# Seven block products for eight in the up-projection of a convolutional FFN, and the FFN in two phases

## What is computed

```python
h = rms_norm(x, norm_ffn[l])
x = x + conv_ffn(h, w_up[l], conv_w[l], conv_b[l], w_down[l])
...
def conv_ffn(h, w_up, conv_w, conv_b, w_down):
    z = causal_dwconv(h @ w_up, conv_w, conv_b)      # width 3, per channel
    val, gate = jnp.split(z, 2, axis=-1)
    return (jax.nn.gelu(gate) * val) @ w_down
```

## Time and profile before

| | us |
|---|---|
| runs of the kernel (three) | 2732.2, 2735.0, 2736.9; median 2735.0 |
| profiled execution, its own time | 2736.5 |
| its span, first to last instruction | 2734.4 |
| TensorE busy | 2628.5, 12338 matmuls and transposes |
| VectorE busy | 1347.1 |
| GpSimd busy | 851.6 |
| ScalarE busy | 693.7 |

### The profile page before, as it was taken

One profiled execution on the slowest core, in us unless ns is written; L12 is line 12 of the kernel. 1 busy time (PEld: TensorE's weight loads), 2 busy tenths in 40 slices (PEclk: granted clock), 3 DMA queues, 4 the chain that ended last, 5 costly groups with the idle time before them and its releaser, 6 DMA issues.

```text
span 2734.4 us, 32749 instructions
## 1 busy us (share of the span) xinstructions
PE 2628.5 (96%) x12338; PEld 2152.5 (79%) x12338; DVE 1347.1 (49%) x1763; ACT 693.7 (25%) x1272; POOL 851.6 (31%) x448
## 2 busy tenths in 40 slices
PE   4999999999999999999999999999999999999997
PEld 3887788887888888888878878888778888888885
DVE  7924455623555555555550335563345455555555
ACT  3126214212222222222241441331232222222222
POOL 1421222531433333333323212236033333333330
PEclk9999999999999999999999999999999999999998
DMA  5342342430111111111123224335011111111111
GB/s 179 95 102 92 128 140 96 148 114 24 62 47 46 46 46 46 46 46 46 65 84 109 70 99 149 111 123 185 1 47 53 48 46 48 52 46 47 52 46 61
DMA packets 87375, 211.34 MB, mean 77 GB/s; under 512 B 15048, under 2 KB 32232, under 8 KB 87288
## 3 DMA queue, kind: packets, MB, share of 16 engines
q1 hardware_dynamic: 47504, 127.02, 14.4%
q10 hardware_dynamic: 39784, 83.10, 8.7%
HBM read 172.87 MB, written 37.22 MB: 77 GB/s over the span
## 4 chain that ended last, share of the span: by engine, by line
PE 89%; DVE 6%; ACT 2%; issue 2%; ACTq 0%; DMA 0%; DVEq 0%; SPq 0%
PE ps L332 28%; PE ps L334 28%; PE ps L333 27%; DVE z L1214 2%; DVE act_lo L936 1%; ACT z L833 1%; PE ps L1467 1%; PE ps L1453 1%; DVE xres L1233 1%; PE ps L1402 1%; PE ps L1391 1%; PE ps L1470 1%; PE ps L1468 1%; PE ps L1318 0%; DVE glu_y L1170 0%
## 5 line engine op out<-in xcount | busy, mean ns | idle before, releaser
L332 PE MATMUL ps<-act_hi,w_hi 128*128 128x512 f32 x2240 | 883.1, 394 | 15.3 <-DVE act_lo L936 11.4
L334 PE MATMUL ps<-act_hi,w_lo 128*128 128x512 f32 x2240 | 875.8, 391 | 0.0
L333 PE MATMUL ps<-act_lo,w_hi 128*128 128x512 f32 x2240 | 875.1, 391 | 0.0
L458 POOL CAST w_hi<-w_raw 128x1024 fp32r<-128x1024 f32 x164 | 184.0, 1122 | 1778.3 <-PE ps L334 1736.7
L332 PEld LDWEIGHTS ps<-act_hi,w_hi 128*128 128x128 f32 x2240 | 422.9, 189 | 106.6 <-DVE act_lo L936 13.0
L334 PEld LDWEIGHTS ps<-act_hi,w_lo 128*128 128x128 f32 x2240 | 422.6, 189 | 89.5
L333 PEld LDWEIGHTS ps<-act_lo,w_hi 128*128 128x128 f32 x2240 | 423.1, 189 | 86.3
L1214 DVE SCALAR_TENSOR_TENSOR z<-pre,conv_v,z 128x1024 f32<-128x1024 f32 x88 | 180.1, 2047 | 523.8 <-ACT z L833 523.8
L460 POOL TENSOR_TENSOR w_lo<-w_raw,w_hi 128x1024 fp32r<-128x1024 f32 x164 | 423.7, 2584 | 13.1
L1233 DVE TENSOR_TENSOR xres<-xres,ps 128x512 f32<-128x512 f32 x352 | 232.7, 685 | 125.2 <-PE ps L334 125.2
L332 PE MATMUL ps<-wd_hi,ff_hi 128*128 128x512 f32 x640 | 251.4, 393 | 26.7 <-DVE xres L1233 26.7
(11 more groups left out here) (271 smaller groups left out, 2992.9 us busy)
## 6 DMA issues: line engine op xcount, KB each, us to landing
w_raw<-in_wu SPq DMA_DIRECT2D x220, 512.0 KB, 3.6
gates<-junk ACTq DMA_DIRECT2D x64, 256.0 KB, 2.0
sig<-gates ACTq DMA_DIRECT2D x32, 512.0 KB, 5.4
tbl_o<-tables ACTq DMA_DIRECT2D x32, 384.0 KB, 3.3
tbl_r<-tables ACTq DMA_DIRECT2D x32, 256.0 KB, 2.7
xres<-in_x ACTq DMA_DIRECT2D x8, 1024.0 KB, 9.6
out<-xres ACTq DMA_DIRECT2D x16, 512.0 KB, 2.8
xin<-in_x SPq DMA_DIRECT2D x4, 1024.0 KB, 8.7
```

The source lines that it names most:

```text
L332: nc.tensor.matmul(out, lh, rh, start=first, stop=False)
L333: nc.tensor.matmul(out, lh, rl, start=False, stop=False)
L334: return nc.tensor.matmul(out, ll, rh, start=False, stop=last)
L458: nc.gpsimd.tensor_copy(hi, w_raw[b][:, :]).then_inc(hi_made, 1)
```

## The change

The FFN of a block is now done in two phases, up and down.

**Up.** A value tile and its gate tile form a pair. With A11, A12 the two K halves of the value weights, A21, A22 those of the gate weights, and the tokens in two halves of 512, the 2x2 block product is made with seven block products (12 matmuls each) in place of eight, from four sums of weight quarters and four of token quarters. VectorE makes the weight sums S1 to S4; GpSimd casts all seven quarters, and makes the low parts of the plain ones, W11, W12 and W22; VectorE makes those of the sums. Each of the seven has one slot. ScalarE copies three partial results out of PSUM, VectorE adds three results (c11, c22, c12) to them, ScalarE reads the fourth (c21). Two sets of three banks alternate. `ff` tiles go to DRAM.

**Token quarters.** The norm's gain is now multiplied in token order (`ffn_scaled`), in `xres` itself; so each raw tile is first stored to DRAM (`x2`), and VectorE waits for the store. VectorE makes four sums per tile and its partner (`token_sum`), TensorE transposes 28 operand tiles for 16 before (`operands`).

**Down.** Two passes over 22 tiles, each for 512 tokens: eight banks accumulate over a whole pass, and VectorE adds them to `xres`, reloaded from `x2`, at its end. `w_down` is loaded and split in both passes (44 splits a block for 22). ScalarE and VectorE split the reloaded `ff` tiles. The next block's norm is done within this phase.

Cores of the diff (buffers, semaphores and counters left out):

```diff
@@ GpSimd
+                for j in (W11, W12, S1, S2):
+                    half(j, 0, 0)
+                pool.wait_ge(o_done, (blk + 1) * TT)
+                for j in (S3, S4, W22):
+                    half(j, 0, 0)
+                half(W11, 0, 1)
+                half(W12, 0, 1)
+                def half(j, i, c):
...
+                    if not isinstance(i, int) or c:
+                        pool.wait_ge(*item(prod_done, j, blk, i, c - 1))
+                    if j == W22:
...
+                        pool.wait_ge(*item(slot_ready, S4, blk, i, c))
...
+                    nc.gpsimd.tensor_copy(slot_hi[j][:, :, :], src).then_inc(slot_half[KIND[j]], 1)
+                    if j in (W11, W12, W22):
+                        pool.wait_ge(*item(slot_half, j, blk, i, c))
+                        nc.gpsimd.tensor_tensor(slot_lo[j][:, :, :], src, f(slot_hi[j][:, :, :]), ALU.subtract).then_inc(slot_ready[KIND[j]], 1)
+                def period(i, c):
+                    here = isinstance(i, int)
+                    if not here or c:
+                        half(W22, i, c)
+                    if not here or c + 1 < FT:
+                        half(S1, i, c + 1)
+                        half(S2, i, c + 1)
+                    if not here or c + 2 < FT:
+                        half(W11, i, c + 2)
+                        half(W12, i, c + 2)
+                    if not here or c + 1 < FT:
+                        half(S3, i, c + 1)
+                        half(S4, i, c + 1)
@@ SP
+                load_pair(0, 0)
+                for i in range(TT):
+                    if i == TT - 1:
+                        sp.wait_ge(o_done, (blk + 1) * TT)
+                        load_pair(0, 1)
+                    sp.wait_ge(o_evac, blk * TT + i + 1)
+                    sp.dma_start(x2[:, i, :], xres[:, i, :]).then_inc(x2_st, 16)
+                def period(i, c):
+                    sp.wait_ge(*item(slot_ready, W22, blk, i, c))
+                    load_pair(i, c + 2)
+                    if not isinstance(i, int) or c:
+                        store_ff(blk, i, c - 1)
@@ ScalarE
+                operand_hi(8, 16)
+                first_partial(0, 0)
+                operand_hi(16, 20)
+                conv_row(0, 0)
+                fifth_partial(0, 0)
+                operand_hi(20, 24)
+                second_partial(0, 0)
+                operand_hi(24, 28)
+                first_partial(0, 1)
+                value_out_pair(0, 0)
+                def period(i, c):
+                    here = isinstance(i, int)
+                    conv_row(i, c)
+                    gate_out_pair(i, c - 1)
+                    fifth_partial(i, c)
+                    second_partial(i, c)
+                    gelu(i, c - 1)
...
+                        first_partial(i, c + 1)
...
+                    value_out_pair(i, c)
@@ VectorE
+                residual(4, 6)
+                ffn_scaled(1)
+                operand_low(0, KD)
+                for t in range(4):
+                    for i in range(2):
+                        token_sum(t, i)
+                residual(6, 7)
+                ffn_scaled(2)
+                for t in range(4):
+                    token_sum(t, 2)
+                residual(7, 8)
+                ffn_scaled(3)
+                for t in range(4):
+                    token_sum(t, 3)
+                slot_low(S3, 0, 0)
+                slot_low(S4, 0, 0)
+                conv_row(0, 0)
+                for m in range(8, OPERANDS, 4):
+                    operand_low(m, m + 4)
```

VectorE's order in a pair c, and TensorE's, with the guards for the first and last pairs cut out:

```diff
+                        conv_row(i, c)
+                        weight_sum(S1, i, c + 1)
+                        near(1, i, c - 1)
+                        slot_low(S1, i, c + 1)
+                        weight_sum(S2, i, c + 1)
+                        far(1, i, c - 1)
+                    c11(i, c)
+                        slot_low(S2, i, c + 1)
+                        ff_mul(i, c - 1)
+                        weight_sum(S3, i, c + 1)
+                        c22(i, c)
+                        slot_low(S3, i, c + 1)
+                        weight_sum(S4, i, c + 1)
+                    c12(i, c)
+                        slot_low(S4, i, c + 1)
+                    near(0, i, c)
+                    far(0, i, c)
@@ TensorE
+                p1(0, 0)
...
+                p2(0, 0)
+                operands(blk, 8, 12)
+                pe.wait_ge(o_evac, (blk + 1) * TT)
+                p1(0, 1)
+                operands(blk, 12, 16)
+                p2(0, 1)
+                operands(blk, 16, 20)
+                pe.wait_ge(f_act, blk * OPERANDS + 12)
+                p5(0, 0)
+                operands(blk, 20, 24)
...
+                def period(i, c):
+                    p5(i, c)
+                    p6(i, c)
+                    if not isinstance(i, int) or c + 1 < FT:
+                        p1(i, c + 1)
+                        p2(i, c + 1)
+                    p7(i, c)
+                    p3(i, c)
+                    p4(i, c)
```

More of the change, by code:

```diff
@@ L53 @@
 U_TABLES = 12
-UNITS = U_FFN + 4 * GROUPS + 2 * GROUPS
-S_UNITS = U_OUT + 4 * GROUPS
+U_UP = U_FFN
+U_DN = U_UP + 2 * FT
+PASSES = 2
+ITEMS = PASSES * FT
+UNITS = U_FFN + ITEMS
+CHUNK = 3
+W11, W12, S1, S2, S3, S4, W22 = range(7)
 TB_W, TB_C, TB_T, TB_V, TB_N = 0, 256, 512, 768, 1280
@@ L328, in leave, with three @@
                 self.reg = None
[L330 to L334, removed]
+        def three(out, lh, ll, rh, rl, first, last, onto=False):
+            nc.tensor.matmul(out, lh, rh, start=first, stop=False, skip_group_check=onto)
+            nc.tensor.matmul(out, lh, rl, start=False, stop=False, skip_group_check=onto)
+            return nc.tensor.matmul(out, ll, rh, start=False, stop=last, skip_group_check=onto)
         def f(ap):
@@ L504, in _ @@
+                for c in range(4):
+                    down_item(0, c)
+                with pool.Fori(1, ITEMS // 4) as i:
+                    for c in range(4):
+                        down_item(i, c)
         @block.scalar
@@ new lines, in operand_low, with c11 @@
+                def operand_low(lo, hi):
+                    for m in range(lo, hi):
+                        dve.wait_ge(fhi_done, blk * OPERANDS + m + 1)
+                        high, low = operand(m)
+                        tt(low, ps[:, operand_bank(m), :], f(high), ALU.subtract).then_inc(f_act, 1)
+                def c11(i, c):
+                    dve.wait_ge(part_out, part_no(1, blk, i, c))
+                    dve.wait_ge(*item(prod_done, W12, blk, i, c))
+                    if later(i, c):
+                        dve.wait_ge(far_done, conv_no(0, blk, i, c - 1))
+                    tt(pre[0][:, 2:2 + HALF], part1[:, :], ps[:, banks(c)[1], :], ALU.add).then_inc(c11_out, 1)
@@ new lines, in _ @@
+                period(0, 0)
+                period(0, 1)
+                with dve.Fori(1, FT // 2 - 1) as i:
+                    period(i, 0)
+                    period(i, 1)
+                period(0, FT - 2)
+                period(0, FT - 1)
+                near(1, 0, FT - 1)
+                far(1, 0, FT - 1)
+                ff_mul(0, FT - 1)
+                with dve.Fori(1, 5) as i:
+                    for c in range(4):
+                        down_low(i, c)
+                if blk + 1 < BLOCKS:
+                    for h in range(2):
+                        norm_x(blk + 1, h)
@@ new lines, in at_pair, with product @@
+                def at_pair(i, c, count=1):
+                    return i * 2 + (blk * FT + c + count)
+                def product(j, i, c, bank, first):
+                    pe.wait_ge(*item(slot_ready, j, blk, i, c))
+                    m0 = {W11: 0, W12: 4, S1: 8, S2: 12, S4: 16, S3: 20, W22: 24}[j]
+                    for k in range(HK):
+                        high, low = operand(m0 + k)
+                        ins = three(ps[:, bank, :], slot_hi[j][:, k, :], slot_lo[j][:, k, :], high, low, first and k == 0, k == HK - 1, not first)
+                    ins.then_inc(prod_done[KIND[j]], 1)
```

927 lines of the change are left out of this document (632 added, 295 removed).

## The result

The changed kernel takes **2685.7 us** (median of 4 runs, 2682.07 to 2687.38) against 2735.7 before (2732.16 to 2736.94): a ratio of 0.9817, 95% interval 0.98 to 0.9834. It is faster, as forecast, but by 50 us (1.8%) and not by 107, and 2685.7 lies above the range of 2592 to 2670. The four times of either kernel lie within 5.3 us of each other, so the gain is clear of the scatter, though it is under 2%.

What follows compares the result with a forecast made beforehand. TensorE, busy 96% of the span, was taken as the bound. 119.9 + 58.3 - 2 x (5.8 + 20.5 + 5 + 4 + 1) + 1.5 = 107.1 us saved gave a median of 2628 us, range 2592 to 2670.

Steps and rivals of the forecast that it cites:

- TensorE's work: FFN: a pair takes 84 matmuls instead of 96, so 528 matmuls at 0.2271 us disappear: 119.9 us saved.
- The old stalls: FFN: all stalls of the old order leave, 25.4 and 32.9 us in the two blocks: 58.3 us saved.
- Ahead of tile 6: Start of the FFN: norm, store and scalings delay the transposes, and the clock falls: 5.8 us more a block.
- Start: After tile 7: store, transposes, low parts and low clock make 20.5 us of excess a block.
- Rest of the up phase: VectorE's lag over the first pairs, 5 us, and steady pairs at 0.2 us a pair, 4 a block.
- Down phase: Splits, reloads and the next block's norm are covered, four tiles ready in advance: 1 us lost a block.
- End: Behind the last matmul only tile 7 and tile 6's norm follow, about 10.2 us for 11.7: 1.5 us saved.
- A: Rival: the port shared by VectorE and GpSimd sets the pace, a pair takes 20.2 us: 2669 us, chance 0.22.
- B: Rival: a cheap start, stores land in 2 us, transposes lie under products, VectorE never lags: 2595 us, chance 0.14.
- C: Rival: slower, VectorE and GpSimd chain without overlap, each pair takes 23.1 us: 2797 us, chance 0.05.
- D: Rival: each pair still lasts the 21.8 us of 96 matmuls: 2739 us, no change, chance 0.02.
- The prediction's rule: VectorE instructions with two SBUF operands and GpSimd's never run together: a 1.28 us step takes 1.94 beside a cast.

Runs made afterwards that it cites:

- e5: Changed kernel with tile 7's store ahead of the second weight pair's load, and VectorE's low parts S3 and S4 ahead of its last scaling: 2673.0 us.
- e4: Changed kernel with c22 of a block's last pair made right behind c11 on VectorE: 2687.1 us.
- e1: Changed kernel with the down phase's eight 1 MB loads issued one at a time behind tiles 6 to 16 on SP: 2665.6 us.
- e2: Changed kernel with the next block's norm done one tile at a time between ff tiles 12 to 22: 2677.8 us.
- e3: Changed kernel with the final norm's four scalings between the low parts of down tiles 25 to 27, stores likewise: 2664.7 us.
- e11: Changed kernel with the edits of e1, e2, e3, e4, e5 and e10, and c12 of the first pair earlier on VectorE: 2613.6 us.
- e7: Changed kernel with GpSimd making all seven low parts of the weight quarters, VectorE none in the up phase: 2734.7 us (one execution).
- e10: Changed kernel with e1, e4 and the loads of down tiles 4 and 5 ahead of the last ff store: 2651.1 us.

## Why the prediction was wrong, point by point

- **TensorE's work**: right. From 720 to 1080 us the up phase runs at 0.2267 a matmul without a hole, 19.04 a pair for the 19.07 of the forecast.
- **The old stalls**: they left, as forecast. No wait for the down products' addition into `xres` stands in the middle of the FFN.
- **Ahead of tile 6**: 5.8 a block forecast, 3.8 and 5.4 measured, as the change in all that stands ahead of the out projection's end. Right.
- **Start**: 20.5 forecast to the first pair's last product, 24.1 and 23.5 measured. The mechanism was right (store, then transposes, then the low clock): the store behind the weight pair landed after 5.60 us where 6.4 was taken, and the last four transposes began 13.1 us (656.44 - 643.36) behind the out projection where 13.8 was taken. The terms that the prediction names for the end of this stretch add up to 45.0 (13.8 + 19.1 + 2.5 + 4 x 2.4) and not to its 47.4, which needs a fifth set of transposes; the 45 that it goes on with is the same. What had no term is the 2.78 us for GpSimd's low part. GpSimd's cast of W22, ahead of it in that queue, was released by VectorE's low part of S4, and in e5, where S3 and S4 come earlier, the wait is gone.
- **Rest of the up phase**: 9 a block forecast as 5 of lag and 4 of steady pairs, 13.2 and 12.0 measured. The steady pairs cost 0, not 4. The lag was there, 3.3 of wait for c21 as described; the 4.62 for c22 **of the last pair**, behind the convolution and the low parts of the first ff tiles, was in no step. The 4 us for the steady pairs hid a part of that by luck.
- **Down phase**: this is the step that failed. The prediction said: "Entry: four tiles are ready in advance, which covers the late stores of the last pair (about 10 us) with 21.8. **1 us a block**", and took reloads and norm as covered. Measured: 35.3 and 14.2. The cover of 21.8 us holds for the store, but only as the last pair itself is 4.62 us late: without that wait (e4) tile 4 waits 5.23 and 3.77. It does not hold from tile 6 on, whose loads stand on SP behind 8 MB of reloads in the first block and 4 MB in the second (e1: 20 us). For the norm the prediction had the price right ("some 6 us", 7.61 measured) and the condition wrong: it asked whether TensorE had work, and not whether that work's own operand was queued on VectorE behind the norm (e2: 8 us). The final norm of the first four token tiles, in the middle of the phase, had no term; it does the same (e3: 21 us): four scalings, 4.87 us at the end of the kernel before, take 10.7 here (from 1257.02 to 1262.43 + 5.34), among GpSimd's splits of down weights. A slack of four tiles at the entry does not help where an in-order queue holds a later tile back. The average was right: with the queues reordered the down phase has no excess (e11).
- **End**: -1.5 forecast, -1.9 measured.
- **Rivals**: A's time, 2669, is nearest to 2685.7, but its mechanism is absent: VectorE and GpSimd do take turns, and TensorE does not notice: it has no wait in the steady pairs. e7 comes nearest to A's picture, with a load in the round besides. B, C and D did not happen.

e11 has the down phase that the forecast described, one with no more than 1 us lost a block, and it took 2613.6 us against 2628. The rest of 14.4 us is mostly the up phase, with 24.8 us of excess a block (25.0 and 24.7) against the 29.5 of the forecast: 2 x 4.7 = 9.4. The difference comes from the edits of e5 and e4, which the forecast kernel does not have; without them the up phase had 37.3 and 35.4.

What stays open: the excess that e11 keeps in the up phase, 18.3 and 16.8 us up to the first pair's last product and 6.7 and 7.9 behind it, was not divided further by a run, between transposes, the low clock and the waits at the start.

## What to carry to other kernels

Where a phase has slack on average, walk each in-order queue once through the phase: a bulk transfer or a norm set between two tiles holds back every later tile of that queue by up to its whole length, less what is ready ahead at that point, whichever engine has time to spare. Split such bulk work into pieces that stand one behind a tile; here that gave 49 us for three edits of order. An edit that only starts a phase sooner shows its worth once the phase's data come sooner too (e4 alone 0, in e10 part of 14.5), so remove waits from the last one backwards or test them together.

## What the runs showed of the hardware

- VectorE and GpSimd do not exclude each other for the whole of an instruction. In e7 the step at 939.21 ends at 941.52, the subtraction beside it at 940.43: 1.09 us behind it for a step of 1.28 alone. The prediction's rule ("each ends where the other's end plus its own length says") is 0.19 us too long there, and it is the same in every one of the 49 steps between 740 and 1080 us that found a GpSimd instruction running (1.08 us behind its end each time), as far as the profile's spans of GpSimd tell. The prediction's own rows have it too: the step at 920.44 ends 1.07 us behind the cast at 919.68. Over a pair, seven casts and seven subtractions (13.3) and VectorE's four sums, four steps and one product (0.6, 1.2 and 1.15 from start to start, 8.3) sum to 21.6 us, and e7's pair takes 20.40, with 2.23 of it a wait for a load. The Trainium skill's page "SBUF — State Buffer" (SBUF: two separate sides) calls the shared port an exclusive lock, held for the whole instruction. By that e7's pair would last at least 21.6; the measurement is shorter, so part of each instruction lies beside the other's. The cast that begins at 940.38 says the same: it ends 0.47 us behind the step, and takes 0.61 alone.
- GpSimd does 128x512 in 0.61 us (cast) and 1.29 (subtraction) alone, in e7. The prediction's 7.7 us a pair for seven casts and three subtractions were 8.1.
- SP's queue takes longer to issue a load while large ones are under way: the first of the eight 1 MB loads took 0.43 us (1114.41), the seventh 3.11 (1119.83; 5.51 with the eighth), before any of them had landed. So the burst delayed what follows twice: tile 6's load was issued at 1127.78 instead of right behind tile 5's at 1113.93, and then took 15.81 us for 3.6. In the second block, behind 4 MB, such a load took 12.21.
